# A modulation row loaded in column quarters, with the first weight chunks between them, and summed rows as 128x2048 pieces

## What is computed

```
cond = jax.nn.silu(c)
for i in range(DEPTH):
    mod = cond @ mod_w[i] + mod_b[i]
    shift, scale, gate = jnp.split(mod, 3, axis=-1)
    h = rms_norm(x, norm_g[i]) * (1.0 + scale[:, None, :]) + shift[:, None, :]
    ...
    x = x + gate[:, None, :] * out
```

## Time and profile before

| | us |
|---|---|
| median of 3 runs | 2357.99 |
| lowest and highest run | 2357.73, 2362.30 |
| profiled execution, its own time | 2359.24 |
| span of its instructions | 2357.0 |
| mean granted TensorE clock | 0.993 |

### The profile page before, as it was taken

The page is one execution under the profiler, slowest core; times in us unless marked ns, Lnnn a source line. Parts: engine busy times, 40 slices in busy tenths (PEclk is TensorE's granted clock), DMA queues, the critical chain, the costliest instruction groups (busy, mean ns, idle before and its releaser), DMA issues.

```text
span 2357.0 us, 29852 instructions
## 1 busy us (share of the span) xinstructions
PE 2310.9 (98%) x10728; PEld 1874.2 (80%) x10728; DVE 1531.7 (65%) x1863; ACT 1134.5 (48%) x1371; POOL 297.5 (13%) x597
## 2 busy tenths in 40 slices
PE   5999999999999999999999999999999999999998
PEld 1877778888788878888888888888888888888886
DVE  2988888666697566775765444665665565565566
ACT  1544444444444456545455444454544444444444
POOL 0000000033300003200031000210231121121120
PEclk8999999999999999999999999999999999999999
DMA  9999996567698547766465766665666666666663
GB/s 391 387 381 373 375 399 253 182 197 222 206 391 274 173 149 235 227 184 183 140 205 169 239 190 194 213 197 188 194 216 204 200 213 197 207 213 195 208 209 112
DMA packets 263659, 547.14 MB, mean 232 GB/s; under 512 B 30188, under 2 KB 30452, under 8 KB 259576
## 3 DMA queue, kind: packets, MB, share of 16 engines
q1 hardware_dynamic: 241520, 510.40, 65.3%
q0 software_dynamic: 20368, 32.58, 4.2%
q10 hardware_dynamic: 1656, 2.66, 0.3%
HBM read 520.36 MB, written 6.30 MB: 223 GB/s over the span
## 4 chain that ended last, share of the span: by engine, by line
PE 89%; DVE 4%; ACT 2%; DMA 2%; issue 1%; POOL 1%; ACTq 0%; DVEq 0%
PE ps L2112 28%; PE ps L2114 28%; PE ps L2113 28%; DMA ifb<-in_f_bias 1%; DVE w_lo L1176 1%; PE ps L2196 1%; PE ps L2230 1%; POOL T L499 1%; PE ps L2409 1%; DMA T<-T 0%; ACT w_hi L568 0%; PE ps L2450 0%; PE ps L2309 0%; PE ps L2386 0%; ACT tmp L898 0%
## 5 line engine op out<-in xcount | busy, mean ns | idle before, releaser
L1176 DVE TENSOR_TENSOR w_lo<-raw,w_hi 128x1024 fp32r<-128x1024 f32 x784 | 945.5, 1216 | 564.2 <-ACT w_hi L568 549.9
L568 ACT CAST w_hi<-raw 128x1024 fp32r<-128x1024 f32 x784 | 814.9, 1046 | 849.6 <-PE ps L2114 801.2
L2112 PE MATMUL ps<-w_hi,xa_hi 128*128 128x512 f32 x2176 | 854.3, 393 | 6.1 <-DVE w_lo L1176 5.0
L2114 PE MATMUL ps<-w_hi,xa_lo 128*128 128x512 f32 x2176 | 847.3, 389 | 0.0
L2113 PE MATMUL ps<-w_lo,xa_hi 128*128 128x512 f32 x2176 | 846.9, 389 | 0.0
L2112 PEld LDWEIGHTS ps<-w_hi,xa_hi 128*128 128x128 f32 x2176 | 408.5, 188 | 100.8 <-issue 9.7
L2114 PEld LDWEIGHTS ps<-w_hi,xa_lo 128*128 128x128 f32 x2176 | 408.4, 188 | 85.6
L2113 PEld LDWEIGHTS ps<-w_lo,xa_hi 128*128 128x128 f32 x2176 | 408.6, 188 | 83.1
L499 POOL DMA_DIRECT2D T<-T x576 | 282.2, 498 | 1182.7 <-DVE T L1276 1029.1
L2112 PE MATMUL ps<-w_hi,xb_hi 128*128 128x512 f32 x928 | 364.2, 392 | 0.9 <-DVE w_lo L1176 0.5
L2114 PE MATMUL ps<-w_hi,xb_lo 128*128 128x512 f32 x928 | 361.3, 389 | 0.0
(11 more groups left out here) (273 smaller groups left out, 1004.1 us busy)
## 6 DMA issues: line engine op xcount, KB each, us to landing
raw<-in_w_in SPq DMA_DIRECT2D x176, 512.0 KB, 4.0
T<-in_mod_w SPq DMA_DIRECT2D x160, 512.0 KB, 7.8
raw<-in_attn_w_in SPq DMA_DIRECT2D x144, 512.0 KB, 4.6
raw<-in_w_up SPq DMA_DIRECT2D x128, 512.0 KB, 4.3
raw<-in_w_down SPq DMA_DIRECT2D x128, 512.0 KB, 4.7
raw<-in_pool_w_in SPq DMA_DIRECT2D x64, 512.0 KB, 8.5
T<-T POOLq DMA_DIRECT2D x576, 32.0 KB, 3.8
T<-in_mod_w SPq DMA_DIRECT2D x16, 1024.0 KB, 9.1
```

What stands on the lines that cost most here:

```text
L568: nc.scalar.copy(w_hi[:, o % SPL, :, 0:cols], raw[:, o % RAW, :, 0:cols]).then_inc(hi_ready, 1)
L1176: tt(w_lo[:, o % SPL, :, part], raw[:, o % RAW, :, part], w_hi[:, o % SPL, :, part].bitcast(F32), ALU.subtract).then_inc(lo_ready, 1)
L2112: mm(dst, x_hi, h, start=first and k == 0, stop=False)
L2114: ins = mm(dst, x_lo, h, start=False, stop=last and k == KPC - 1)
```

## The change

- **Scale row of layer 0 in quarters.** The row is now loaded as 32 pieces of 128 x (2 x 512), 512 KB each, quarter of the columns by quarter, in six slots. In each quarter the last two pieces are followed by the next two weight chunks of pool_v. PE multiplies a piece by 8 matmuls of 128 columns (`quarter_piece`) where it was 4 of 512 for 1 MB; after each quarter come a copy, one turn to columns, two small operations and ACT's and DVE's parts of a quarter of the input (`quarter_scale`, `quarter_columns`). PE runs chunks 0 and 1 after quarter 0, then all of quarter 1, then chunks 2 and 3, and so on to chunk 7.
- **x first.** x comes through SP's queue ahead of the row, in two transfers of 1 MB. DVE's rotary angles move behind the first quarter.
- **Rides of 128 x 2048.** `rider` adds one piece of 128 x 2048 in one operation; there are two slots. The rides start at chunk 8 instead of 4; all 32 pieces for PE now come in pool_gate and pool_out.
- **Sums to rows.** The sum of unit 0 is taken three chunks later in group, and its shift follows later. `total` is gone; unit 3 goes through `total_rows`, a copy of DVE and `mod_columns`. The transposes of norm1 also follow an idle stretch that waits for the root.
- **mix_out by tiles.** In its last block PE finishes chunks 4 to 7 for token tile 0 and then for tile 1. DVE and ACT take tile 0 while PE works on tile 1; DVE's multiplication of tile 1 moves behind the residual sums.

```diff
@@ -63,16 +64,16 @@
 
 RIDERS = {"gate": 5}
 CLEARED = {u: i + 1 for i, u in enumerate((2, 0, 3, 5))}
-RIDE = {u: 2 * KC * i for i, u in enumerate((0, 2, 3, 5))}
+RIDE = {u: KC * i for i, u in enumerate((0, 2, 3, 5))}
 
 
 def _rides():
     first = {name: PHASES[name][0] * CPB for name in ("pool_v", "group", "pool_gate")}
     v, gate = first["pool_v"], first["pool_gate"]
-    at = [v + c for c in range(4, 32) for _ in range(2 if c in (11, 17, 23, 28) else 1)]
+    at = [v + c for c in range(8, 36) for _ in range(2 if c in (11, 17, 23, 28) else 1)]
     at += [gate + i * 9 // 8 for i in range(32)]
     at += [gate + 36 + i * 27 // 32 for i in range(32)]
-    return at, [first["group"] + i for i in range(8)] + [gate + 1 + i * 60 // 24 for i in range(24)]
+    return at[1::2], [gate + 1 + i * 60 // 32 for i in range(32)]
 
 
...
 
             mws = [mod_w[i].rearrange("(p k) (u n) -> p u k n", k=KC, n=D) for i in range(2)]
             sp.dma_start(csil[:], c[0].rearrange("(p k) -> p k", k=KC)).then_inc(c_landed, 16)
-            for k in range(KC):
-                if k >= 4:
-                    sp.wait_ge(mod_taken, k - 3)
-                sp.dma_start(mod_raw[:, k % 4, :], mws[0][:, 1, k, :]).then_inc(mod_landed[k % 4], 16)
+            for t, arrived in enumerate((x_landed, x_second)):
+                sp.dma_start(T0[:, t, :], x[0, t * P:(t + 1) * P, :]).then_inc(arrived, 16)
+            for m in range(M0):
+                if m >= 6:
+                    sp.wait_ge(mod_taken, m - 5)
+                i, col = m % 8, m // 8 * NBLK
+                sp.dma_start(mod_raw[m % 6].rearrange("p (k n) -> p k n", k=2), mws[0][:, 1, 2 * i:2 * i + 2, col:col + NBLK]
+                             ).then_inc(mod_landed[m % 6], 16)
+                if i >= 6:
+                    load(SOURCES["pool_v"], 0, m // 8 * 2 + i - 6, 0, first=True)
...
+            def ride(u, b, i):
+
+                sp.wait_ge(mod_used, b * 4 + (RIDE[u] + i - 1))
+                sp.dma_start(ride_raw[:, i % 2:i % 2 + 1, :], whole(u, b, i)).then_inc(ride_landed[i % 2], 16)
...
+            def quarter_scale(q):
+
+                bank, part = 3 - q % 2, slice(4 * q, 4 * q + 4)
+                dve.wait_ge(mod_taken, 8 * q + 8)
+                nc.vector.tensor_copy(q_raw[:, q * P:q * P + P], ps[:, bank, 0:P]).then_inc(q_rows, 1)
+                dve.wait_ge(q_sum, q + 1)
+                step(tt(scl[:, 0, part], ps[:, bank, S:S + 4], MODB[0][:, part], ALU.add))
+                step(tt(scl[:, 0, part], scl[:, 0, part], G0[:, part], ALU.mult))
+                dve.sem_inc(q_scl, 1)
+                norm0_low(q)
+
             lo(0, 0)
-            scale(0, 1, ps[:, 2, 0:KC], G0)
-            norm0_low(0)
+            quarter_scale(0)
             lo(0, 1)
-            norm0_low(1)
+            rotary_angles()
+            rotary_turns(cos, 0.25)
+            rotary_last()
             lo(0, 2)
+            quarter_scale(1)
             B0 = PHASES["pool_v"][0]
             for b in range(4):
                 first_blk(B0 + b, {6: lambda: low_job(SPLITS["pool_v"] + b - 1, XB, b - 1, 4)} if b else
-                          {3: lambda: norm0_low(2), 5: lambda: norm0_low(3)})
+                          {4: lambda: quarter_scale(2), 6: lambda: quarter_scale(3)})
 
...
             first_blk(PHASES["group"][0], {
-                4: shift_rows, 5: shift0_start, 6: lambda: shift0_next(0),
-                7: lambda: shift0_next(1), 8: lambda: shift0_next(2), 9: lambda: shift0_next(3)})
+                4: lambda: low_job(SPLITS["pool_v"] + 3, XB, 3, 4), 7: shift_rows, 8: shift0_start,
+                9: lambda: shift0_next(0), 10: lambda: shift0_next(1)})
+            shift0_next(2)
+            shift0_next(3)
 
...
+                dve.wait_ge(mix_tile, 1)
+                mix_last(0)
+                dve.sem_inc(mix_part, 1)
+
+            blk(B0 + n - 1, {7: mix_tile_scaled})
...
+            def quarter_piece(q, i):
+
+                m = 8 * q + i
+                pe.wait_ge(mod_landed[m % 6], 16 * (m // 6 + 1))
+                for k in range(2):
+                    col = csil[:, 2 * i + k:2 * i + k + 1].to_broadcast([P, 32])
+                    for r in range(4):
+                        at = k * NBLK + r * P
+                        ins = mm(ps[32 * r:32 * r + 32, 3 - q % 2, 0:P], col, mod_raw[m % 6][:, at:at + P],
+                                 start=i == 0 and k == 0, stop=i == 7 and k == 1, skip_group_check=True)
+                ins.then_inc(mod_taken, 1)
+
+            def quarter_columns(q):
+
+                pe.wait_ge(q_rows, q + 1)
+                mm(ps[:, 3 - q % 2, S:S + 4], q_raw[:, q * P:q * P + P], ident[:, 0:P:32], start=True, stop=True
+                   ).then_inc(q_sum, 1)
+
             pe.wait_ge(csil_ready, 1)
-            for k in range(KC):
-                mod_piece(k, mod_raw[:, k % 4, :], 3, 0, NBLK, mod_landed[k % 4], 16 * (k // 4 + 1), k == 0)
-                if k == 7:
+            for i in range(8):
+                quarter_piece(0, i)
+                if i == 3:
                     pe.wait_ge(vec_landed, 16 * 13)
                     pe.wait_ge(con_landed, 16)
                     nc.tensor.transpose(ps[:, 4, 0:104], stage[0:104, 0, 0:P], ident[0:104, 0:104])
                     nc.tensor.transpose(ps[:, 5, 0:96], stage[0:96, 1, 0:P], ident[0:96, 0:96]).then_inc(vec_tp, 1)
-                if k == 11:
+                if i >= 3:
+                    awake(1)
+                if i == 5:
                     pe.wait_ge(vec_done, 1)
-                    hooks.pop(-1)()
-                if k > 11:
-                    awake(2 if k < KC - 1 else 4)
-            mod_columns(1, 2, 0, False)
-            awake(5)
+                    norm_job("norm0", 0, xn, 0)
+                if i == 6:
+                    norm_job("norm0", 0, xn, 1)
+            quarter_columns(0)
...
+            for j in range(CPB):
+                if j == 0:
+                    pe.wait_ge(x_first, 1)
+                else:
+                    pe.wait_ge(x_ready, SPLITS["norm0"] + j // 2 + 1)
+                chunk(0, j, XA, KPC * j, 0, j == 0, j == CPB - 1)
+                if j in (0, 2):
+                    norm_job("norm0", 0, xn, 2 + j // 2)
+                if j in (1, 3, 5):
+                    q = (j + 1) // 2
+                    if q >= 2:
+                        pe.wait_ge(q_scl, q - 1)
+                    for i in range(8):
+                        quarter_piece(q, i)
+                    quarter_columns(q)
+            B0, A0, n = PHASES["pool_v"]
+            blk(B0 + 1, A0 + 1, XA, False, {3: lambda: pool(0)})
+            with pe.Fori(2, n) as b:
+                blk(b + B0, b + A0, XA, True, {3: lambda: pool(b - 1)})
             B0, A0, _ = PHASES["group"]
...
@@ -2320,11 +2375,11 @@
                 chunk(B0, j, XB, KPC * j, A0 + j // 2, j % 2 == 0, j % 2 == 1)
                 if j == 0:
                     pool(3)
-                if j == 1:
+                if j == 4:
                     pe.wait_ge(tp_evac, JOBS["pool_v"] + 3)
                     total_rows(0, 6)
-                if j == 2:
-                    mod_columns(2, 6, 0, False)
+                if j == 5:
+                    mod_columns(1, 6, 0, False)
                 mod_rides(B0 * CPB + j)
             XA, XB = SECOND, FIRST
...
+            def by_tiles(B, A, X, tile):
+
+                pe.wait_ge(acc_free, A - 1)
+                for j in range(4):
+                    chunk(B, j, X, KPC * j, A, j == 0, False)
+                for t in range(NT):
+                    for j in range(4, CPB):
+                        chunk(B, j, X, KPC * j, A, False, j == CPB - 1, (t,),
+                              w_used if t else tile if j == CPB - 1 else None)
...
 
-            total(3, 6, 0)
-            mod_columns(3, 7, KC, True)
+            total_rows(3, 6)
+            mod_columns(2, 7, KC, True)
             awake(4)
+            mod_columns(3, 6, 0, False, mod_rows2)
+            pe.wait_ge(root_ready, 2)
+            awake(3)
             norm_job("norm1", 1, T1, 0)
-            pe.wait_ge(scl_ready, 2)
+            pe.wait_ge(scl_ready, 1)
```

194 lines of the change are left out of this document (93 added, 101 removed).

## The result

| | before | after |
|---|---|---|
| median of its runs | 2357.86 us | 2387.45 us (2386.08 to 2388.80, four runs) |
| after / before | | 1.0126, 95% interval 1.0113 to 1.0138 |
| span of the profiled execution | 2357.0 us | 2384.3 us |

The change costs 29.6 us. The prediction was 2367 with a range of 2352 to 2380, so the time lies 7 us above the range: the direction was right, the size three times too small (9.3 against 29.6).

What follows compares the result with a forecast made beforehand. PE was taken as the bound, busy 98% of the span. Start +9.8, group +2.7, rides 0, norm1 -2.3 and mix_out -0.9 gave +9.3 us on the median 2358.0: 2367.3 us, range 2352 to 2380.

Steps and rivals of the forecast that it cites:

- Rides and DMA: Merged rides, and more transfers per chunk in pool_out: no change, 0, with +4 us as upper end.
- the end of quarter 0: Start: the first quarter's last piece at 23.5 us (22 to 28), chunk 0 starting at 26.7.
- the clock: Start: 1 us added for each of three returns to chunks after PE's waits (0 to 2.7 each).
- a quarter's pieces: Start, quarters 1 to 3: eight pieces take 8.3 us, PE waiting for pieces 14 and 15 to land.
- (a): The forecast itself: three exposed cycles of chain and refill in the start, 2367 us; chance 0.60.
- The chain: Start, behind quarters 1 to 3: copy, columns, small operations, ACT and DVE leave PE nothing queued for 5.0 us.
- (d): Rival: all six chunks after the returns at 1.2 GHz, and late rides holding up DVE in pool_out; 2384 us, chance 0.08.
- Group: Later shift of unit 0 without covering pieces makes PE wait at pool_gate's start: +2.7 us (0 to 4).
- Norm1: After pool_out: replacing `total` by `total_rows` brings the transposes earlier, -2.3 us (0 to -3.5).
- Mix_out: End of mix_out: with tile 0 done beforehand the sum comes one square earlier, -0.9 us (0 to -1.2).
- (b): Rival: the overlap pays, with chunk 8 at 81 us and a faster kernel at 2352 us; chance 0.18.

Runs made afterwards that it cites:

- warm: Changed kernel plus idle matmuls wherever PE waits in the start, ahead of late pieces and behind turns to columns; 2385.6 us.
- pipe8: Changed kernel with PE's order interleaving pieces of the next quarter with chunks, and eight slots for quarter pieces instead of six; 2363.7 us.
- half_warm: Changed kernel plus idle matmuls in the start's waits, loading only half the columns of each ride of units 0, 2 and 3; 2375.6 us.
- half_after: Changed kernel loading only half the columns of each ride of units 0, 2 and 3, operations unchanged; 2382.7 us.
- pe8: Changed kernel with eight of PE's pieces back between group's chunks and the other 24 at their former places; 2383.5 us.
- move8: Kernel before with one edit: none of PE's pieces in group, all 32 in pool_gate and pool_out; 2361.0 us.
- old_start: Changed kernel with the former start: scale row whole and ahead of chunk 0, all else of the change kept; 2366.2 us.
- best: Changed kernel with interleaved quarters, eight piece slots, rides of 128x1024 in four slots, and PE's pieces at former places in group; 2359.0 us.
- rides2048: Kernel before with one edit: rides as pieces of 128x2048 in two slots, one operation per pair; 2358.0 us.

## Why the prediction was wrong, step by step

Two steps failed. "Rides and DMA", which the sum held at nothing, cost 5.0 us; and in the start three terms were too small, the end of quarter 0 (+4.1), the clock (+2.9) and a quarter's pieces (+2.6). The mechanism of forecast (a), three exposed cycles of chain and refill, was there.

- **Quarter 0** was put at 23.5; its last piece started at 27.04 and ended at 27.68 us, near my upper end of 28. Up to 20.0 us PE still waited for transfers: 6.4 MB had come by then and not 7.4 (310 and 331 GB/s in the first two windows of 10 us). From there on it had no such wait and was busy to the end: pieces at 1.08 each up to 22.8, the transposes between them, and the idle matmuls, which I had left out. (1.08 is what a piece cost at a clock of 0.64 later, at 45.78; for 11 to 23 us the windows say 1.00, so that the low clock is read from the durations only.) PE's first piece waited until 11.55 for silu(c), which ACT now does behind 18 issues of transfers, at 11.28 instead of 3.53; the description of the change left that out. The waits for transfers that came behind it make it unlikely that this set the end. I took the time from bytes (7.3 MB) where PE's queue was last. +4.1 at chunk 0.
- **A quarter's pieces**: 8.3 forecast, 9.5, 8.5 and 9.5 measured (first piece to end of the last). The mechanism is right, with the wait for pieces 14 and 15; but the second wait of each cycle was 3.3, 2.1 and 3.1 us where the sum had piece 15 two transfers of 1.35 us behind piece 14, 2.0 us of waiting at a piece of 0.72. The piece itself was priced too high, 0.72 against 0.47 (0.64 alone, 1.08 cold). +2.6 in all.
- **The chain**: 5.0 forecast, 4.8 measured three times. Right, -0.6 in all.
- **The clock** was priced at half: 1 us for each return, 1.9, 1.4 and 2.6 measured, so 6 us instead of 3. The row of 40 to 45 us in the earlier trace rows had shown it, I called the whole price the upper end and had put it into rival (d), at 0.08. The Trainium skill ("TensorE: Matmul & The Clock Gate", section "HAM oscillation — how this bites in real kernels") says that in a kernel whose bursts of matmuls are separated by DMA waits every burst starts cold; chunks 2, 4 and 6 agree with it in kind (here the stop ahead of them is that of the chain), but only chunk 6 ran cold to its end. By its rule the start would have been 5 us above my sum, and half of the start's miss would be gone. warm shows the price of the clock by an experiment: 6.8 us at chunk 8, the cold last pieces of the quarters included.
- **Group**: the stall was forecast at 2.7 and was 2.66, `w_lo`, the ride of 2.34 us and the low part in the forecast order. The input was ready 15.8 us after chunk 4 of group, as forecast; that the stall came out so near is partly luck, since 15.8 and my 12.7 for PE differ by 3.1. Its consequence wasn't forecast: chunk 40 behind it ran cold (4.3 us; 14.1 us from chunk 40 to 44 against 12.5 before), +1.6. Six of the kernels with this stall took 14.1 to 14.2 us there, and warm, pipe8 and half_warm 12.9, so a stop of 2.7 us doesn't always bring the cold chunk.
- **Rides and DMA: 0**. My own sum had 3.5 us of DMA for each chunk of 3.1 us in pool_out, and I set it aside because the eight slots of `raw` had absorbed the like before. They don't here. The eight moved pieces don't only move PE's 5.7 us; they ask for 4.2 MB in a stretch whose DMA share was 1.04 already. What that costs, waits and the cold chunk behind them, is 5.0 us (210.5 against 205.5 of half_after), above my upper end of 4. It needs both the pieces and the bytes: with the pieces back in group (pe8) 40 to 103 took 198.9, and 2.4 of the 5.0 go with four slots. The 12.9 us are then these 5.0, chunk 40 with 1.6, and 6.3 for the eight pieces: between two chunks of pool_gate a piece costs 0.79 us (3.38 and 2.85 from start to start instead of 2.72 each), a little more than the 5.7 that group lost.
- **Norm1**: -2.3 forecast and -2.5 in the trace, but that is luck: the reference trace had that stretch at the low clock, as move8 shows.
- **Mix_out**: from the idle matmuls behind the last chunk to the reduction of the sums it was 2.0 us before (to 1641.18) and 1.2 after; -0.8 there, as forecast. But the forecast stopped at the root. The feed-forward part keeps the 0.8 us up to its chunk 3 and loses them at chunk 4: DVE's multiplication of tile 1, which the change moved behind the residual sums, stands ahead of `w_lo` (0.7 us), and PE waits for it. DVE and PE after, then PE at the same chunk before:

```profile
1678.96 0.68 DVE L2016 TENSOR_TENSOR T<-ps,wide 128x512 f32<-128x512 f32 x1
1685.29 2.36 DVE L1189 TENSOR_TENSOR w_lo<-raw,w_hi 128x1024 fp32r<-128x1024 f32 x2
1686.66 0.47 PE L2139 MATMUL ps<-w_hi,xb_hi 128*128 128x512 f32 x1 [0.69 <-DVE w_lo L1189]
```

```profile
1659.69 0.48 PE L2112 MATMUL ps<-w_hi,xb_hi 128*128 128x512 f32 x1
```

From the idle matmuls on, that is 20.6 us after against 20.5 before. From chunk 104 to the end the four kernels with the old code took 1957.3 to 1958.2 us and the thirteen with the new one 1957.4 to 1959.5: the -0.9 isn't there. That the moved multiplication is what takes it back is read from the order and not run apart.

- **The rivals**: (d) had both mechanisms, and its 2384 was the nearest number, partly by luck: it had 13 us more than my sum for the clock, where 2.9 were measured, and nothing for quarter 0, the pieces and chunk 40. (b), the overlap that pays, failed on its chunk 8 (102.8 against 81); and where pipe8 reached 78.7 the time was still 2364, because the rest of the change costs 7.7 us by old_start, and because an early start needs DMA to be idle somewhere later, and there is no such place up to 155 us.

## What to carry to other kernels

Before moving work ahead, add up the bytes as well as the engine time: where the transfers were full for the next 100 us, an engine that started earlier waited later for most of what it had won (2.7 of 4.1 us in pipe8). Shorter rows seem to push it further back (364 against 392 GB/s in best), so a row that is needed before anything else can start is better loaded in long rows, though no run here cut it into quarters with long rows. If it is cut, PE's order has to interleave it with the work it releases (24 us here for a reordering of one engine). And add to each stop of PE the cold chunk that can follow it: 1.4 to 2.6 us behind the stops of 4.8 us here, and some 1.6 behind that of 2.7 us in six kernels of nine. A gain at the end of a phase counts only if it is still there some chunks into the next.

## What the runs showed that I had not expected

- The same norm1 code took 12.9 to 15.6 us in four kernels; where it took 15.6 the granted clock was 0.68 and 0.54, where it took 12.9 it was 0.97 and 0.75. A gain read from one trace in a stretch with short PE work can be that.
- An operation of DVE of 128x2048 with a column scalar took 2.34 us against 2.56 for two of 1024, and the saving bought nothing: rides2048 is at 1.0000.
- Full DMA engines moved 386 GB/s in the quartered start of pipe8 (30 to 60 us) and 409 in the same stretch of before, both at a share of 1.03 to 1.05.
